# A mixture-of-experts encoder layer on one core: experts of at most 64 tokens stacked in one stationary operand, large and small experts in one loop

## The reference

```python
def swiglu(x, w_gate, w_up, w_down):            # 1024 -> 3584 -> 1024 for an expert
    return (jax.nn.silu(x @ w_gate) * (x @ w_up)) @ w_down

def moe_swiglu(x, w_router, w_gate, w_up, w_down):
    logits = (x @ w_router).astype(jnp.float32)
    top_v, top_i = lax.top_k(logits, TOP_K)     # TOP_K = 2
    gates = jax.nn.softmax(top_v, axis=-1)
    combine = jnp.sum(jax.nn.one_hot(top_i, N_EXPERTS, dtype=jnp.float32) * gates[..., None], axis=-2)
    ...
    for e in range(N_EXPERTS):
        out = out + combine[..., e:e + 1].astype(x.dtype) * swiglu(x, w_gate[e], w_up[e], w_down[e])
```

## Time and profile before

| | |
|---|---|
| median of 3 runs | 1437.84 us (1437.79 to 1438.27) |
| span of the profiled execution, first to last instruction | 1436.7 us |
| TensorE busy | 1358.7 us, 95% |
| VectorE busy | 884.7 us, 62% |
| ScalarE busy | 697.8 us, 49% |
| from the first matmul of the experts to their last addition | 857.3 us |

### The profile page before, as it was taken

How to read it: one execution, slowest core, us unless ns; L and a number is a source line. 1 busy time by engine, 2 the same in 40 slices (tenths; PEclk the granted TensorE clock), 3 DMA queues, 4 the chain that set the end, 5 groups by cost and what they waited for, 6 DMA issues and landing times.

```text
span 1436.7 us, 16475 instructions
## 1 busy us (share of the span) xinstructions
PE 1358.7 (95%) x6328; PEld 1122.1 (78%) x6328; DVE 884.7 (62%) x789; ACT 697.8 (49%) x690; POOL 58.3 (4%) x48
## 2 busy tenths in 40 slices
PE   7799999999989995999999999999999999999995
PEld 5678878888767885888888788888878878887874
DVE  3757555454675745545453545454488889878886
ACT  3445334433444622434433434433377677767772
POOL 3000110000410000000000000000000000000000
PEclk9895899999999586999999999999999999999998
DMA  9821265555570005755555555555579989998991
GB/s 272 301 85 61 86 211 192 183 176 177 151 233 16 1 0 190 269 191 193 182 177 194 170 195 194 183 180 189 188 275 379 370 290 363 378 333 313 382 369 54
DMA packets 126746, 299.84 MB, mean 209 GB/s; under 512 B 4923, under 2 KB 7113, under 8 KB 126689
## 3 DMA queue, kind: packets, MB, share of 16 engines
q1 hardware_dynamic: 124016, 290.47, 58.4%
q0 software_dynamic: 2384, 7.92, 2.2%
q10 hardware_dynamic: 288, 0.63, 0.1%
HBM read 297.88 MB, written 1.12 MB: 208 GB/s over the span
## 4 chain that ended last, share of the span: by engine, by line
PE 82%; DVE 7%; issue 4%; ACT 3%; DMA 2%; POOL 1%; DVEq 0%; POOLq 0%; SPq 0%; ACTq 0%
PE bank L1121 25%; PE bank L1122 25%; PE bank L1179 16%; PE bank L1207 8%; ACT w_hi L490 2%; PE bank L1224 2%; DVE w_lo L707 2%; DMA raw<-in_w_in 1%; DVE soft L779 1%; PE bank L1327 1%; PE bank L1431 1%; DVE neg_max L780 1%; POOL w_lo L449 1%; PE bank L1314 1%; PE bank L1135 1%
## 5 line engine op out<-in xcount | busy, mean ns | idle before, releaser
L707 DVE TENSOR_TENSOR w_lo<-raw,w_hi 128x2048 fp32r<-128x2048 f32 x273 | 629.9, 2315 | 438.2 <-ACT w_hi L490 437.3
L490 ACT ACTIVATE w_hi<-raw 128x2048 fp32r<-128x2048 f32 x275 | 524.7, 1918 | 438.7 <-PE bank L1179 218.0
L1121 PE MATMUL bank<-w_hi,xT_hi 128*128 128x512 f32 (+1 forms) x1232 | 483.8, 394 | 8.8 <-DVE xT_lo L719 3.2
L1122 PE MATMUL bank<-w_hi,xT_lo 128*128 128x512 f32 (+1 forms) x1232 | 477.4, 388 | 0.0
L1179 PE MATMUL bank<-w_lo,xT_hi 128*128 128x512 f32 (+1 forms) x1168 | 308.8, 387 | 0.2 <-DVE w_lo L707 0.2
L1121 PEld LDWEIGHTS bank<-w_hi,xT_hi 128*128 128x128 f32 x1232 | 233.0, 189 | 56.7 <-ACT xT_hi L501 6.1
L1122 PEld LDWEIGHTS bank<-w_hi,xT_lo 128*128 128x128 f32 x1232 | 233.0, 189 | 45.5
L1179 PEld LDWEIGHTS bank<-w_lo,xT_hi 128*128 128x128 f32 x1168 | 217.5, 188 | 45.6 <-DVE w_lo L707 0.6
L1121 PE MATMUL bank<-w_hi,hT_hi 128*128 128x512 f32 x480 | 191.2, 398 | 2.9 <-DVE hT_lo L875 1.5
L1122 PE MATMUL bank<-w_hi,hT_lo 128*128 128x512 f32 x480 | 190.3, 396 | 0.0
L1207 PE MATMUL bank<-w_lo,hT_hi 128*128 128x512 f32 x480 | 131.8, 396 | 0.0
(11 more groups left out here) (178 smaller groups left out, 688.3 us busy)
## 6 DMA issues: line engine op xcount, KB each, us to landing
raw<-in_moe_w_gate SPq DMA_DIRECT2D x70, 1024.0 KB, 5.3
raw<-in_moe_w_up SPq DMA_DIRECT2D x70, 1024.0 KB, 5.6
raw<-in_moe_w_down SPq DMA_DIRECT2D x70, 1024.0 KB, 5.0
raw<-in_w_in SPq DMA_DIRECT2D x24, 1024.0 KB, 11.3
raw<-in_ffn_w_gate SPq DMA_DIRECT2D x11, 1024.0 KB, 5.2
raw<-in_ffn_w_up SPq DMA_DIRECT2D x11, 1024.0 KB, 5.2
raw<-in_ffn_w_down SPq DMA_DIRECT2D x11, 1024.0 KB, 4.9
raw<-in_w_out SPq DMA_DIRECT2D x8, 1024.0 KB, 5.1
```

Source lines behind the costliest of these rows:

```text
L490: nc.scalar.activation(w_hi[:, n % NH, :], raw[:, n % NR, :], ACT.Copy).then_inc(hi_done, 1)
L707: nc.vector.tensor_tensor(w_lo[:, n % NH, :], raw[:, n % NR, :], w_hi[:, n % NH, :].bitcast(F32), ALU.subtract).then_inc(lo_done, 1)
L1121: nc.tensor.matmul(o, hi, wh, start=start, stop=False)
L1122: nc.tensor.matmul(o, lo, wh, start=False, stop=False)
```

## The change

**Threshold.** `SMALL = 64` takes the place of 128: an expert is large with over 64 tokens. At most 64 gathered tokens fill half a tile, so their high parts stand in columns 0 to 63 and their low parts in columns 64 to 127 of one stationary operand (`xs`, and `hs` for the hidden values). One pass with `w_hi` gives hi·hi in rows 0 to 63 and lo·hi in rows 64 to 127, one with `w_lo` adds hi·lo: 8 matmuls for a unit, not 12. The halves must be added before silu and before the product: ScalarE copies rows 64 to 127 out of the bank (`small_half`), VectorE adds them to rows 0 to 63 (`small_gate`, `small_up`). For the output no addition is made: `sel` has the token in both halves, and the scatter sums them.

**One loop for two experts.** The loop `PAIR` runs once for each large expert and takes a small one with it (a dummy where there is none). Its 84 units alternate. Small experts left over run in the loop `REST` of 42 units. With the router's counts above there are two `PAIR` iterations and one `REST` iteration.

**Places.** The gains of LayerNorm go to `acc` (to `raw` for the last one), `lam_in` and the router's table move to memory that is freed later, and `lam_in` is loaded for each layer. The gather uses 64 columns. The routing code has two more small VectorE instructions and four memsets. Nothing else changes ahead of the experts.

The units of a `PAIR` iteration (`L` large, `S` small):

```diff
+def pair_units():
+
+    order = []
+    for c in range(len(MOE_W)):
+        for kind in ("gate", "up"):
+            order += [("L", kind, c, 0), ("L", kind, c, 1), ("S", kind, c, 0), ("S", kind, c, 1)]
+    small = 0
+    for i in range(N_DOWN - 2):
+        order.append(("L", "down", i, 0))
+        for _ in range(0 if i == 0 else 1 if i < 9 else 2):
+            order.append(("S", "down", small, 0))
+            small += 1
+    assert small == N_DOWN
+    return order + [("L", "down", N_DOWN - 2, 0), ("L", "down", N_DOWN - 1, 0)]
```

ScalarE, a helper and the loop over units:

```diff
+            def small_half(c, kind, cs, used):
+
+                act.wait_ge(unit_used, used)
+                if kind == "up":
+                    act.wait_ge(s_gate, cs + (c + 1))
+                elif c > 0:
+                    act.wait_ge(s_up, cs + c)
+                nc.scalar.activation(hid_s[SMALL:P, :], bank[SMALL:P, 6 if kind == "gate" else 7, :],
+                                     ACT.Copy).then_inc(s_half, 1)
...
+                for u, (who, kind, c, part) in enumerate(units):
+                    n = BASE_MOE + u
+                    if (who, kind, part) == ("L", "gate", 1):
+                        act.wait_ge(unit_used, n + 1 + off)
+                        large_gate(c, cb)
+                        if c > 0:
+                            hidden_hi(c - 1, MOE_W, len(FFN_W), range(NT), item * NCH)
+                            small_hidden_hi(units, c - 1, cs)
+                    if who == "S" and kind != "down" and part == 1:
+                        small_half(c, kind, cs, off + (n + 1))
+                    if u + NH < n_units:
+                        split_hi(n + NH, off, use)
+                    if (who, kind, part) == ("S", "gate", 1):
+                        small_gate(c, cs)
+                        if units is REST and c > 0:
+                            small_hidden_hi(units, c - 1, cs)
```

VectorE, the same:

```diff
+            def small_up(c, cs):
+
+                dve.wait_ge(s_half, cs * 2 + (2 * c + 2))
+                nc.vector.tensor_tensor(bank[0:SMALL, 7, :], bank[0:SMALL, 7, :], hid_s[SMALL:P, :],
+                                        ALU.add).then_inc(s_up, 1)
+                dve.wait_ge(s_up, cs + (c + 1))
+                dve.wait_ge(s_silu, cs + (c + 1))
+                nc.vector.tensor_tensor(hid_s[0:SMALL, :], hid_s[0:SMALL, :], bank[0:SMALL, 7, :],
+                                        ALU.mult).then_inc(s_hid, 1)
...
+                    if (who, kind, part) == ("L", "up", 1):
+                        large_up(c, cb, used)
+                    if (who, kind, part) == ("S", "gate", 1):
+                        small_gate(c, cs)
+                    if (who, kind, part) == ("S", "up", 1):
+                        small_up(c, cs)
+                    if u + NH < n_units:
+                        split_lo(BASE_MOE + u + NH, off)
+                    if (who, kind, part) == ("L", "gate", 1) and c > 0:
+                        hidden_lo(c - 1, MOE_W, len(FFN_W), range(NT), item * NCH)
+                    if (who, kind, part) == (units[0][0], "gate", 1) and c > 0:
+                        small_hidden_lo(units, c - 1, cs)
+                    if (who, kind, c, part) == ("S", "gate", 0, 1):
+                        scatter_matrix(item)
+                        select(item + 1)
```

TensorE, the same:

```diff
+            def small_columns(n, part, b, off):
+
+                nk = KT // 2
+                pe.wait_ge(hi_done, off + (n + 1))
+                for w, ready in ((w_hi, None), (w_lo, lo_done)):
+                    if ready is not None:
+                        pe.wait_ge(lo_done, off + (n + 1))
+                    wv = w[:, n % NH, :].rearrange("p (k n) -> p k n", k=nk)
+                    for k in range(nk):
+                        kt = part * nk + k
+                        ins = nc.tensor.matmul(bank[:, b, :], xs[:, kt, :], wv[:, k, :],
+                                               start=kt == 0 and ready is None, stop=kt == KT - 1 and ready is not None)
+                ins.then_inc(unit_used, 1)
...
+                    elif who == "S" and kind == "gate":
+                        if part == 0 and c == 0:
+                            pe.wait_ge(g_lo, item + 1)
+                        elif part == 0:
+                            pe.wait_ge(s_gate, cs + c)
+                        elif c > 0 and not large:
+                            pe.wait_ge(s_hid, cs + c)
+                        small_columns(n, part, 6, off)
+                    elif who == "S" and kind == "up":
+                        if part == 0 and c > 0:
+                            pe.wait_ge(s_lo, cs + c)
+                        small_columns(n, part, 7, off)
+                    elif who == "S":
+                        if c == 0:
+                            pe.wait_ge(s_lo, cs + (NCH if large else NCH - 1))
...
+                        if c == 1 and not large:
+                            pe.wait_ge(s_hid, cs + NCH)
...
+                        small_rows(n, c, small_out(units), off)
+                    if (who, kind, c, part) == ("S", "gate", 0, 1):
+                        transpose_sel(done)
+                        if large:
+                            pe.wait_ge(selT_in, item + 1)
+                    if who == "L" and ((kind == "gate" and part == 1 and c > 0) or (kind == "down" and c == 0)):
+                        chunk = c - 1 if kind == "gate" else NCH - 1
+                        pe.wait_ge(s_hid, cs + (chunk + 1))
+                        large_transposes(chunk, cb)
+                        small_transposes(units, chunk)
+                    if not large and ((kind == "gate" and part == 1 and c > 0) or (kind == "down" and c == 1)):
+                        small_transposes(units, c - 1 if kind == "gate" else NCH - 1)
```

More of the change, by code:

```diff
@@ L103, in shape_table @@
     put("ident", np.eye(P))
-    put("iota", np.tile(p, (P, 1)))
+    put("iota", np.tile(p % SMALL, (P, 1)))
     put("before", p[:, None] < p[None, :])
@@ L382, in _ @@
             n_large = sp.value_load(work[0:1, AT_LARGE:AT_LARGE + 1], min_val=0, max_val=MAX_LARGE)
[L383 to L391, removed]
-                    load(BASE_MOE + u, src.rearrange("o (k p) n -> p (o k) n", p=P), off)
-                for i in range(F_EXP // 256):
-                    src = moe_w_down[0, bass.ds(e, 1), i * 256:(i + 1) * 256, :]
-                    load(BASE_MOE + len(cols) + i, src.rearrange("o (k p) n -> p (o k) n", p=P), off)
+            n_rest = sp.value_load(work[0:1, AT_REST:AT_REST + 1], min_val=0, max_val=NE)
@@ L694, in _ @@
+                    run_units(PAIR, act.snap(r * U_PAIR), act.snap(r * (16 * U_PAIR // NR)), r, r + 1 < n_items)
+            with act.If(n_rest > 0):
+                with act.Fori(0, n_rest) as i:
+                    off = act.snap(n_large * U_PAIR + i * U_REST)
+                    use = act.snap(n_large * (16 * U_PAIR // NR) + i * (16 * U_REST // NR))
+                    run_units(REST, off, use, act.snap(n_large + i), i + 1 < n_rest)
         @block.vector
@@ L1436, in _, with gather @@
-            with pe.If(n_small > 0):
-                gather(0)
+            n_rest = pe.value_load(work[0:1, AT_REST:AT_REST + 1], min_val=0, max_val=NE)
+            def gather(item):
+                pe.wait_ge(sel_ready, item + 1)
+                for kt in range(KT):
+                    for tt in range(NT):
+                        ins = nc.tensor.matmul(bank[:, 4, kt * SMALL:(kt + 1) * SMALL], xtok[:, tt, kt * P:(kt + 1) * P],
+                                               sel[:, tt, 0:SMALL], start=(tt == 0), stop=(tt == NT - 1))
+                ins.then_inc(gather_psum, 1)
@@ new lines, in scatter @@
+            def scatter(item, tt, done):
+                if tt == 0:
+                    pe.wait_ge(selT_in, item + 1)
+                    pe.wait_ge(y_lo, item * 2 + 2)
+                    pe.wait_ge(g_lo, item + 2)
+                else:
+                    pe.wait_ge(added, done)
+                for ch in range(2):
+                    for y, stop in ((yo_hi, False), (yo_lo, True)):
+                        ins = nc.tensor.matmul(bank[:, 4 + ch, :], selT[:, tt, :], y[:, ch * CW:(ch + 1) * CW],
+                                               start=not stop, stop=stop)
+                    ins.then_inc(scatter_psum, 1)
```

526 lines of the change are left out of this document (323 added, 203 removed).

## The result

| | us |
|---|---|
| after, median of 4 runs | 1422.07 (1418.87 to 1423.2) |
| before, median of 4 runs | 1437.82 (1436.29 to 1438.27) |
| ratio | 0.9885, 95% interval 0.9872 to 0.9898 |

The account below looks back on a forecast made before the run. TensorE was taken to bound the experts, VectorE next. Two pairs at 339.8 us plus `REST` at 158.3 gave 837.9 against 857.3, -19.4; with -1.1 at the start, 1417.3 us was forecast, range 1399 to 1436.

Parts of the forecast that it names:

- two `PAIR` iterations: Both paired loops: 339.8 us each from work, refill and `selT` wait, 679.6 together, a gain of 53.
- waits for `selT` with the clock behind them: First chunk of each pair: TensorE idle 8.7 us until VectorE's copy, plus 1.7 at half speed; 10.4 a pair.
- refill behind the small gate pair: Six of seven chunks a pair: high and low parts for the large up unit late, 1.1 us each, 6.6 a pair.
- the gather: Start of each pair: taken as 16 matmuls at 1.6 us, from 6.2 for 32 at the low clock.
- work alone: One pair without waits: large expert 239.1 us, small units 77.2, transposes, scatter and gather; sum 322.8.
- `REST`, to its last addition: Loop of the unpaired small expert: first chunk 15.7, six more 106.8, down phase 29.6, end 5.6; 158.3 us, losing 34.
- a chunk of it: One `REST` chunk, old 11.3 us: 17.8 with low clock behind the wait for the subtraction to `hs`, 15.7 at full clock.
- start of the expert part: Ahead of the first unit: shorter gather gains 1.5 us, routing is 0.4 later; -1.1.
- a gather of 16: Term of a pair's work: 16 gather matmuls, half of half of 6.2 us, 1.6.
- The rival of the clock: `REST`: TensorE stays at 1.2 GHz between gaps throughout, giving 1428 us; chance 0.09.
- The slower case: `PAIR`: large unit behind each small pair waits 2.29 us at 26 column places, 60 us, giving 1477; chance 0.13.
- The covered case: Full clock in `REST` (-12.6) and no wait behind gate pairs (-13), giving 1391 us; chance 0.11.

Follow-up runs that it names:

- run 1: Changed kernel with TensorE's wait for the `selT` copy moved to the second chunk's transposes in `PAIR`: 1404.16 us, 0.9753 of before.
- run 3: Changed kernel with ScalarE's split for the large up unit put ahead of its copies to `hT_hi` and `hs`: 1415.03 us, 0.9829 of before.
- run 8: Changed kernel with the edits of run 1, run 2 and run 3 together: 1361.2 us, 0.9465 of before.
- run 7: Changed kernel with unused matmuls in both gaps of `REST` chunks, 20 behind the small transposes and 9 behind the first gate unit: 1414.08 us.
- run 6: Changed kernel with 20 unused matmuls behind the small transposes of each `REST` chunk, one gap only: 1421.04 us, 0.9871 of before.
- run 2: Changed kernel with the transposed hidden values in `REST` in a bank of their own (5, not 7): 1391.27 us, 0.9666 of before.
- run 5: Kernel before with only the descriptor scratch size for GpSimd's DMAs set to 4096: 1433.42 us against 1439.32, ratio 0.9967.

## Why the prediction was right, and where it was off

The forecast of the span was 20.5 us less; 15.5 came. The terms of the sum and what was measured:

| term | predicted | measured |
|---|---|---|
| two `PAIR` iterations | 679.6 | 343.9 + 341.6 = 685.5 |
| of these, waits for `selT` with the clock behind them | 2 x 10.4 | 2 x 10.3 (run 1, net) |
| of these, refill behind the small gate pair | 12 x 1.1 | 12 x 0.78 (run 3) |
| of these, the gather | 2 x 1.6 | 2 x 3.68 |
| work alone, one pair | 322.8 | 326.4 (run 8, second pair, idle time left out) |
| `REST`, to its last addition | 158.3 | 159.2 |
| a chunk of it (mean of six), and at the full clock | 17.8, 15.7 | 17.7, 15.75 (run 7) |
| start of the expert part | -1.1 | -2.9 |

**`PAIR`.** Both stalls were where the walk had put them, and experiments 1 and 3 took them out one by one. The chain of the `selT` copy was walked to 12.5 us behind the start of the small gate units and gave 8.7 of idle time; two times 8.5 were measured. That 10.4 a pair met 10.3 is luck in part: the clock was put at 1.7 and cost 2.8, and the refill of the first chunk, which the sum leaves out, is hidden by the wait and comes back for 1.0 when the wait is gone (run 1). The refill was 0.3 us a chunk too dear. What failed is the sum "work alone", 322.8: with all waits but 0.6 us gone, run 8 still takes 328.8 and 327.0. The term named wrong is "a gather of 16". It has 32 matmul records, as many as before, each with half the columns, and hardly faster. Timelines of before and of after, at the full clock:

```profile
1139.97 3.73 PE L1431 MATMUL bank<-sel,xtok 128*128 128x128 f32 x32
```

```profile
1182.29 3.68 PE L1598 MATMUL bank<-sel,xtok 128*128 128x64 f32 x32
```

That is 2.1 us in each pair. As much comes from the small column units: in the second pair of run 8 the 28 of them take 53.0 us from start to start, 1.87 or 1.88 each and 1.98 behind the transposes, where 1.82 each, 51.0, had been put. The transposes of `sel` take 0.8 there, with 0.4 of idle time, and not 0.2. The large expert's units and transposes are 239.0 there and had been put at 239.1, although a set of eight transposes now takes 0.96 (in after, 959.85 to 960.81) in place of 0.79. The first pair has 2.3 more than the second in after, since its first twelve matmuls run at the low clock (564.02 to 569.00, 5.0 us in place of 2.7).

**`REST`.** The total was right to 0.9 us, and its parts nearly so: the first chunk 15.3 us for 15.7, the six 106.5 for 106.8, and 37.5 from the last product to the last addition for 35.8. The walk gave 15.7 us at full clock; with TensorE kept busy the chunk is 15.75. So the clock costs 2.0 us a chunk, where 2.1 had been put. The additions on 64 rows cost 0.68 and 0.69 us, no less than 128 rows did; by this, the trace agrees with the Trainium skill (VectorE: DVE Perf Modes, "Why `tensor_reduce` can't reduce along partition axis").

**The rival of the clock.** The granted clock didn't stay low through `REST`; it was 0.81 in the chunk shown, and full speed came back in the third pass behind the gap. The Trainium skill (TensorE: Matmul & The Clock Gate, "HAM oscillation — how this bites in real kernels") describes a kernel in which every burst between waits begins slowly; the rows of after have that behind the gap of 5.25 us and not behind that of 1.58, which is followed by four matmuls in 1.20. With the long gap filled, the short one's unit did begin slowly (run 6). Which of the gaps pays isn't settled by the gap's length alone: run 2 has both a full-speed and a half-speed unit behind 3.20 us. What settles it stays open; that filling both gaps brings 10.5 us of `REST` is shown.

**The other rivals.** The slower case needed 0.9 us at each of 26 places; the refill cost 0.78 at 12 (run 3). The covered case needed both a `REST` of 158.3 - 12.6 = 145.7 and no wait behind the gate pairs, and neither came: `REST` has 159.2, and it takes filler matmuls to come near its value (148.0 in run 7).

**The start.** Here the result was near for a wrong reason. The gather was to be shorter, with 1.5 us gained; at the low clock it took 7.09 us against 6.22, and the clock rose later (the granted clock is 0.50 until 568 us in after, where before has 0.99 in the us from 566). Timeline of after:

```profile
557.17 7.09 PE L1598 MATMUL bank<-sel,xtok 128*128 128x64 f32 x32 [8.58 <-DVE sel L1141]
564.02 0.77 PE L1290 MATMUL bank<-w_hi,xT_hi 128*128 128x512 f32 x1
```

The gain comes from ahead: the gather begins 3.8 us sooner than before. The text ahead of the prediction says that nothing else changes ahead of the experts, and the sum has no term for the descriptor memory, which does change there; run 5 puts 4.7 us on it. The forecast owes part of its nearness to this: without these 4.7 us the change would give some 11 us, an estimate from 15.75 and run 5, and not 20.5. This gain isn't steady: in the profiles of the eight other kernels made from after, the gather begins between 556.8 and 561.3 us, and in that of run 5 at 554.3. What moves it between executions stays open.

## What to carry to other kernels

Stacking two operand halves takes a third of the matmuls away, but the two units that a slot's refill has for cover then last less (3.7 us) than the refill (4.45), so each instruction between two units on another engine becomes visible: walk those chains first, and give each handover a bank of its own, which was worth twice the change itself. Interleave short units with long ones where the long ones can cover the short ones' chains; here the one iteration that has no partner lost 34 of the 47 us that the others gained, nearly all of it to the shared bank. Where a loop stops TensorE in two places, price the clock by filling both, since filling one moved the slow matmuls to the other.

## What was not expected of the hardware

- 32 float32 matmuls with 64 columns took 3.68 us and with 128 columns 3.73; at the low clock 7.09 and 6.22, the latter with the clock rising towards its end.
- A filler of 20 matmuls (4.96 us) moved the half-speed unit from one gap of the loop to the other. The length of the idle time doesn't tell which unit it is: the four matmuls took 1.20 us and 1.99 us behind the same 3.20 us of idle time in two chunks of run 2.
- The descriptor memory set to 4096 delayed a DMA's issue by 13 us and made the kernel before 4.7 us faster (run 5).
